# First layer's attention: transposes and masks, then all scores, then all values of two groups in each step; five buffers of probabilities

## What is computed

```python
s_cmp = einsum(q, kc) * scale;  p_cmp = masked_softmax(s_cmp, cmask);  o_cmp = p_cmp @ vc
# selected blocks: 4 blocks of 64 tokens, top 16, so all causal keys are taken
s = einsum(q, ks) * scale;      p = masked_softmax(s, causal);         o_slc = p @ vs
o_win = banded_attention(q, kw, vw, 512)      # the window covers all 256 tokens
gates = sigmoid(gt + gate_b)
o = gates[0] * o_cmp + gates[1] * o_slc + gates[2] * o_win
x = x + from_q_groups(o) @ w_o
```

## Time and profile before

| What | Value |
| --- | --- |
| Median of 3 runs | 1122.2 us (1118.98 to 1123.57) |
| Span of the profiled execution, its own time | 1119.2 us |
| TensorE busy | 1095.6 us, 98% of the span |
| VectorE, ScalarE, GpSimd busy | 731.5, 574.7, 449.2 us |
| Mean granted TensorE clock | 0.997 |
| The attention stage of the first layer | about 92 to 143 us of the span |

### The profile page before, as it was taken

One profiled execution on the slowest core, in us unless ns is written; L12 is line 12 of the kernel. 1 busy time (PEld: TensorE's weight loads), 2 busy tenths in 40 slices (PEclk: granted clock), 3 DMA queues, 4 the chain that ended last, 5 costly groups with the idle time before them and its releaser, 6 DMA issues.

```text
span 1119.2 us, 23474 instructions
## 1 busy us (share of the span) xinstructions
PE 1095.6 (98%) x9175; PEld 1048.5 (94%) x9175; DVE 731.5 (65%) x1029; ACT 574.7 (51%) x827; POOL 449.2 (40%) x430
## 2 busy tenths in 40 slices
PE   7999999999999999999999999999999999999998
PEld 6897799999999869999999999999998989999997
DVE  6776757777555866877746564558747668777543
ACT  5546755544443665555535447645346445544333
POOL 4464714666402661666622112213533014666300
PEclk9999999999999999999999999999999999999999
DMA  9740147766555416666645454243334445766552
GB/s 286 248 129 23 40 133 209 196 184 184 187 170 170 151 43 185 186 189 186 186 163 181 156 184 150 79 151 114 115 112 151 151 114 158 200 181 182 188 181 76
DMA packets 226408, 175.40 MB, mean 157 GB/s; under 512 B 8720, under 2 KB 207632, under 8 KB 226208
## 3 DMA queue, kind: packets, MB, share of 16 engines
q1 hardware_dynamic: 225056, 173.00, 51.3%
q10 hardware_dynamic: 1248, 1.35, 0.4%
q0 software_dynamic: 32, 0.03, 0.0%
HBM read 173.32 MB, written 1.05 MB: 156 GB/s over the span
## 4 chain that ended last, share of the span: by engine, by line
PE 83%; DVE 5%; ACT 4%; POOL 3%; issue 3%; DMA 2%; SPq 0%; DVEq 0%; POOLq 0%; ACTq 0%
PE psum L630 24%; PE psum L636 23%; PE psum L631 23%; PE psum L696 2%; ACT w_h L1423 2%; DVE w_l L1882 1%; PE psum L833 1%; DMA raw<-in_nsa_w_in 1%; PE psum L1268 1%; POOL work L2767 1%; POOL work L2769 1%; PE psum L1100 1%; PE psum L860 1%; PE psum L1355 1%; PE psum L806 1%
## 5 line engine op out<-in xcount | busy, mean ns | idle before, releaser
L630 PE MATMUL psum<-xh,w_h 128*128 128x256 f32 (+3 forms) x1760 | 438.4, 286 | 9.9 <-ACT w_h L1488 7.4
L631 PE MATMUL psum<-xl,w_h 128*128 128x256 f32 (+3 forms) x1760 | 432.3, 283 | 0.0
L630 PEld LDWEIGHTS psum<-xh,w_h 128*128 128x128 f32 (+1 forms) x1760 | 331.6, 188 | 15.3 <-ACT w_h L1488 7.4
L631 PEld LDWEIGHTS psum<-xl,w_h 128*128 128x128 f32 (+1 forms) x1760 | 332.4, 189 | 0.5
L1882 DVE TENSOR_TENSOR w_l<-raw,w_h 128x2048 fp32r<-128x2048 f32 (+2 forms) x91 | 202.7, 2228 | 140.8 <-ACT w_h L1423 140.8
L1423 ACT ACTIVATE w_h<-raw 128x2048 fp32r<-128x2048 f32 x92 | 167.8, 1824 | 202.3 <-PE psum L636 184.4
L636 PE MATMUL psum<-xh,w_l 128*128 128x256 f32 (+3 forms) x1760 | 245.7, 282 | 0.7 <-DVE w_l L1882 0.7
L636 PEld LDWEIGHTS psum<-xh,w_l 128*128 128x128 f32 (+1 forms) x1760 | 224.6, 188 | 1.9 <-DVE w_l L1882 1.2
L2664 POOL TENSOR_TENSOR work<-work 128x256 f32<-128x256 f32 x66 | 160.7, 2434 | 135.5 <-ACT work L1621 135.5
L2201 DVE TENSOR_TENSOR w_l<-raw,w_h 128x2048 fp32r<-128x2048 f32 x66 | 151.4, 2293 | 13.9 <-ACT w_h L1608 13.3
L630 PE MATMUL psum<-hid_h,w_h 128*128 128x256 f32 (+1 forms) x592 | 148.4, 282 | 0.5 <-issue 0.5
(11 more groups left out here) (329 smaller groups left out, 1414.5 us busy)
## 6 DMA issues: line engine op xcount, KB each, us to landing
raw<-in_ffn_w_gu SPq DMA_DIRECT2D x88, 512.0 KB, 5.0
raw<-in_w_in SPq DMA_DIRECT2D x26, 1024.0 KB, 5.0
raw<-in_ffn_w_down SPq DMA_DIRECT2D x40, 512.0 KB, 4.6
raw<-in_w_ffn_up SPq DMA_DIRECT2D x22, 512.0 KB, 3.9
raw<-in_w_ffn_gate SPq DMA_DIRECT2D x22, 512.0 KB, 5.2
raw<-in_w_ffn_down SPq DMA_DIRECT2D x20, 512.0 KB, 4.3
raw<-in_nsa_w_in SPq DMA_DIRECT2D x9, 1024.0 KB, 6.2
raw<-in_swa_w_qkv SPq DMA_DIRECT2D x5, 1024.0 KB, 5.3
```

Of the source, the lines that this page charges most:

```text
L630: mm(dst, parts[0][:, k, cols], high, start=first, stop=False)
L631: mm(dst, parts[0][:, k, cols], low, start=False, stop=False)
```

## The change

The masks are taken out of `first_scores` and `second_scores` into functions of their own. Step i of TensorE's loop becomes: transposes of parts 3i-5 and 3i-4, first masks of group i, transposes of part 3i-3, second masks, first scores, second scores, second values of group i-2, first values of group i-1. Parts of kind 1 and 2 are thus transposed one step later than before. `S_p` gets a fifth buffer. ScalarE, VectorE and GpSimd have their queues put in an order that goes with it; ScalarE's third copy has a function of its own, and the pieces of the weight slabs move. The last two steps' projection products are cut 3 and 2 instead of 2, 1 and 2.

```diff
-        S_p = cv(4, 512)
+        S_p = cv(5, 512)
...
-            def first_scores(ci):
+            def first_masks(ci):
 
                 if ci:
                     pe.wait_ge(at_exp, 3 * ci - 2)
-                pe.wait_ge(roped, 13 if ci < 4 else 14)
                 for a in range(2):
                     mm(bank[4 + a][:, 0:256], ident_b[:, :], each(causal, 2), start=True, stop=False, skip_group_check=True)
+
+            def first_scores(ci):
+
+                pe.wait_ge(roped, 13 if ci < 4 else 14)
...
-            def second_scores(ci):
+            def second_masks(ci):
 
                 if ci:
                     pe.wait_ge(at_exp, 3 * ci)
...
+
+            def second_scores(ci):
+
...
             for i in range(1, 8 + 2):
+                if i >= 2:
+                    part_turn(3 * i - 5)
+                    part_turn(3 * i - 4)
+                if i < 8:
+                    first_masks(i)
                 if i <= 8:
                     part_turn(3 * i - 3)
                 if i < 8:
+                    second_masks(i)
                     first_scores(i)
-                if i == 8:
-                    out_opening(11, (at_out, 0), 0, 2)
-                if i == 9:
-                    out_opening(11, (at_out, 0), 3, 5)
+                    second_scores(i)
+                else:
+                    out_opening(11, (at_out, 0), *((0, 3), (3, 5))[i - 8])
                 if i >= 2:
                     second_values(i - 2)
                 if i <= 8:
-                    part_turn(3 * i - 2)
-                if i < 8:
-                    second_scores(i)
-                if i <= 8:
                     first_values(i - 1)
-                    if i == 8:
-                        out_opening(11, (at_out, 0), 2, 3)
-                    part_turn(3 * i - 1)
...
-                if p >= 4:
-                    act.wait_ge(at_turned, p - 3)
+                if p >= 5:
+                    act.wait_ge(at_turned, p - 4)
...
+            def third_copy(ci):
+
+                p = 3 * ci + 2
+                act.wait_ge(at_turned, p + 1)
+                if p >= 4:
+                    act.wait_ge(at_pv, 2 * ci)
+                line.put(fn(S_pt[:, p % 4, :], bank[p % 2][:, :], ACT.Copy), at_pt_act)
+
             for i in range(8 + 2):
                 if i >= 2:
-                    attention_high(i - 2, True)
+                    third_copy(i - 2)
+                if 1 <= i <= 8:
+                    high_piece(11 + (i - 1) // 4, (i - 1) % 4)
                 if i < 8:
                     part_exp(3 * i)
                 if i == 0:
                     take_cmp()
                     take_values(0)
+                if i >= 2:
+                    attention_high(i - 2, True)
                 if i < 8:
                     part_exp(3 * i + 1)
                 if i == 0:
                     take_values(1)
-                if 1 <= i <= 8:
-                    p = 3 * i - 1
-                    act.wait_ge(at_turned, p + 1)
-                    if p >= 4:
-                        act.wait_ge(at_pv, 2 * i - 2)
-                    line.put(fn(S_pt[:, p % 4, :], bank[p % 2][:, :], ACT.Copy), at_pt_act)
                 if i < 8:
                     part_exp(3 * i + 2)
-                    high_piece(11 + i // 4, i % 4)
...
             for i in range(8 + 2):
+                if i >= 2:
+                    part_copy(3 * i - 5)
                 if 1 <= i <= 8:
                     part_factor(3 * i - 2)
                     part_copy(3 * i - 3)
                     part_factor(3 * i - 1)
-                if 1 <= i < 8:
-                    part_max(3 * i)
-                if 1 <= i <= 8:
-                    part_copy(3 * i - 2)
+                if i < 8:
+                    if i:
+                        part_max(3 * i)
+                    part_max(3 * i + 1)
+                    part_max(3 * i + 2)
+                    if i:
+                        part_factor(3 * i)
                 if i >= 2:
                     attention_low(i - 2, 0, True)
-                if 1 <= i < 8:
-                    part_factor(3 * i)
-                if i < 8:
-                    part_max(3 * i + 1)
-                    part_max(3 * i + 2)
...
-                if p and p % 3 == 0:
+                if p > 2 and p % 3 == 2:
                     low_piece(11 + (p // 3 - 1) // 4, (p // 3 - 1) % 4)
```

## The result

The changed kernel takes 1123.16 us (median of 20 runs, 1120.21 to 1125.68), the kernel before 1120.52 us in 20 runs (1118.59 to 1123.57). The ratio is 1.0023 with an interval of 1.0016 to 1.0031: slower by 2.6 us. The forecast had no difference. The page of the changed kernel's profiled execution shows its span, the busy time of the engines (against the earlier trace rows), and the granted clock in 40 slices of the span.

A forecast was written before the change was run, and what follows sets the result against it. TensorE was taken to bound the stage. Opening +0.75, five steps -0.66 and end -0.12 summed to -0.03 us, giving 1119.2 us for the profiled execution and 1122.2 for the median, range 1118.8 to 1125.2.

The forecast's parts named there:

- the opening: Stage start, up to first scores of group 2: second masks wait for group 0's third exponential, costing 0.75 us.
- the five steps: First scores of group 2 to those of group 7: 29.60 us against 30.26, a gain of 0.66.
- the end: Last first scores to last second values: 11.49 us against 11.61, a gain of 0.12.
- rival B: Opening: TensorE idles 1.8 us in one piece and the clock falls, losing 1.6 us, giving 1123.8; chance 0.10.
- The step of 5.92 us: Steady step: transposes of part 3i-3 wait 0.27 us for their bank, so it takes 0.13 us less than now.
- The hand-over back: Steady step: from the end of VectorE's copy to TensorE's transposes into the freed bank, taken as 0.04 us.
- The savings on TensorE's side: TensorE's own work per step: fewer array-shape changes give 5.60 us, 0.45 less, 3.2 us over seven steps without waits.
- Rival A: Steady steps: the bank is free in time, 0.27 us less in six steps, giving 1120.6; chance 0.10.
- Rival C: Scores: the new order saves no entry or exit, the step is 6.13 us, giving 1123.3; chance 0.07.
- Rival D: VectorE's factor products wait for GpSimd's running instruction: 1136.7, or 1126 at half the full amount; chance 0.03.
- The fifth buffer: Probabilities: without it, exponentials would wait for transposes that now come a step later; it costs no instruction.
- The two edits at nothing: Weight pieces half a step later, at most 1.27 us, and ScalarE's third copy ahead of exponentials: both costed at nothing.

The follow-up runs named there:

- the run with the maxima first: Changed kernel, old order in step 1, second masks before third transposes from step 2, VectorE's maxima and a factor before its copy: 0.9991 of the kernel before.
- the gap added to before: Kernel before, with step 1's first masks and scores also waiting for group 0's third exponential: ratio to the kernel before 1.0019, median 1122.40 us.
- masks first: Changed kernel with the second masks ahead of the third transposes: ratio to the kernel before 1.0031 (1.0020 to 1.0042).

## Why the prediction was wrong, step by step

**The sum at full clock was nearly right.** It came out at -0.03 us. The runs give +0.83 for the opening (12.01 against 11.18; forecast 0.75), -0.21 for the five steps (forecast -0.66) and -0.25 for the end (forecast -0.12): +0.37.

**The step that failed is the opening, which the sum took at full clock, with the fall of the clock left to rival B.** I named it, with its place and the idle piece of 1.8 us (measured 1.74), and gave it 0.10, because the present gaps ran at full clock. But the present gaps are shorter, 0.52 and 1.21 us with scores between, and that they did no harm is no evidence for a longer one. The gap's length was an output of my own sum; I should have treated it as a change of what TensorE does, with a chance near even. Its price was too low as well: 1.6 us from a stretch of 4.00 us at 0.59, where the clock stayed low for 6.75 us and cost 14.41 - 12.01 = 2.40. With 0.37 that makes the 2.77 us of the stage. In medians it is 2.6 us. The sum had no difference from before. That the forecast time of 1122.2 missed 1123.16 by only 1.0 us is luck: it started from the median of three runs, 1.7 us above that of twenty. Why the clock falls behind this gap and not behind one of 1.21 us, the runs do not say.

**The step of 5.92 us was 6.01.** The mechanism was right: the transposes of part 3i-3 wait for VectorE's copy, in every step. (The row's 0.22 us counts from the masks' end. In the forecast's reckoning TensorE is ready 1.15 us into the step and starts at 119.87 - 118.34 = 1.53, a wait of 0.38 for the 0.27 forecast.) The hand-over back was mis-sized. I took 0.04 us from VectorE to ScalarE; from the copy's end (119.03 + 0.69 = 119.72) to TensorE's transposes at 119.87 it is 0.15. That is 0.11 in each step, and it accounts for all of the 0.09 by which the step came out longer.

**The savings on TensorE's side came as worked out.** Both scores take 1.51 us (120.64 to 122.15), two transposes 0.93, masks 0.31. The Trainium skill's drain at a change of tiling mode (TensorEngine Tiling (Array Packing), Key Properties) is again in agreement: the scores of both kinds, now adjacent, follow each other at 0.10 us (120.64 + 0.72 - 0.27 = 121.09, next at 121.19), without the 0.10 more.

**Rival A** did not occur: the wait stayed. **Rival C** did not: scores were cheaper by the change of order. **Rival D** did not in the changed kernel: its factors' products take 0.16 us in the steady steps. In the run with the maxima first one took 1.02 us behind GpSimd's running instruction without harm to the step: the maxima behind it started at 117.63, 0.05 us after the scores' end. The rival's two prices were not reckoned alike, either: 1136.7 counts from the present step of 6.05 us, 1126 from the 5.92.

**The fifth buffer** I took for needed, without a number for it. With four the step was the same. **The two edits at nothing** (the weight pieces, the third copy) cost nothing that a run shows, but no run tries them by themselves.

**The level.** I set the span of 1119.2 us against the times of the runs and put the profiled execution at their low end. In all runs on record the span is 1.7 to 1.9 us below the time of the same run, so by that estimate it took about 1121 us, 2 us above the lowest of the three. No term of the sum hangs on it.

## What to carry to other kernels

When a reordering saves tenths of a microsecond per step, walk through its first step as carefully as the steady one: an idle piece on TensorE that is new or longer costs its own wait plus what the clock may take afterwards, here 0.8 us and another 2.4. The test is cheap: fill the piece with matmuls that nobody reads, and if the time comes back, reorder that one step. And a ring of waits includes the order of every queue that it passes: whoever moves a group on one engine asks what the others now do first.

## What the runs showed of the hardware

In the changed kernel the granted clock fell to the lower level right behind a stretch in which TensorE was busy 1.86 of 3.60 us, with one idle piece of 1.74 us, and stayed there for 6.75 us though TensorE was busy all that time. With idle pieces of 1.96 us (the gap added to before) and 2.18 us (masks first) it fell before the piece had ended and stayed low for about 10.3 and 3.4 us, so the longer piece did not bring the longer low stretch. With idle pieces of at most 1.21 us (before) or 1.10 us (the old order in step 1) it stayed up. With the gap of the changed kernel filled by matmuls that nobody reads it stayed up as well. A wait of TensorE for VectorE's copy ended 0.15 us after the copy's end, while the same kind of release from VectorE to ScalarE took 0.03.
